# Expert blocks of mixed widths (96, 64 and 32 slots side by side) in a mixture-of-experts stage

## What is computed

```python
scores = sigmoid(h @ w_router)
_, idx = lax.top_k(where(expert_mask, scores + router_bias, -inf), TOP_K)   # 8 of 64, from 4 of 8 groups
gate   = scores at idx, divided by their sum, times 2.5
for each expert e, for the tokens that chose it:
    y = (silu(h @ w_gate[e]) * (h @ w_up[e])) @ w_down[e]
    out[token] += gate * y
out += (silu(h @ ws_gate) * (h @ ws_up)) @ ws_down                          # a shared expert, all tokens
x = rmsnorm(x + g2 * out, final_g)
```

## Time and profile before

| | |
|---|---|
| median of 3 runs | 1466.32 us (1465.88 to 1468.25) |
| the profiled execution | 1468.9 us, span 1467.2 us |
| TensorE busy | 1426.4 us, 97% of the span |
| granted TensorE clock, mean | 0.993 |
| the stage of experts, from the first `gate_up` | 951 us to 1455 us |
| loads from HBM in the middle of that stage | 417 to 422 GB/s |

### The profile page before, as it was taken

The page is one execution under the profiler, slowest core; times in us unless marked ns, Lnnn a source line. Parts: engine busy times, 40 slices in busy tenths (PEclk is TensorE's granted clock), DMA queues, the critical chain, the costliest instruction groups (busy, mean ns, idle before and its releaser), DMA issues.

```text
span 1467.2 us, 17841 instructions
## 1 busy us (share of the span) xinstructions
PE 1426.4 (97%) x6990; PEld 887.1 (60%) x6990; DVE 457.5 (31%) x1035; ACT 210.9 (14%) x515; POOL 67.5 (5%) x101
## 2 busy tenths in 40 slices
PE   8999999999999999999999999999999999999985
PEld 7676585675658867577575675744454445444542
DVE  1136442422542355242245063422111111111113
ACT  2135200000002331000012141200000000000001
POOL 1016200000000010000000000000000000000000
PEclk9999999999999999999999999999999999999997
DMA  9721174464264335664634405589999999998993
GB/s 394 293 82 59 58 275 184 143 245 184 86 229 145 115 116 213 248 254 183 243 148 158 152 21 207 206 346 378 421 421 404 422 421 421 418 421 331 422 421 157
DMA packets 51833, 368.45 MB, mean 251 GB/s; under 512 B 5856, under 2 KB 6064, under 8 KB 7984
## 3 DMA queue, kind: packets, MB, share of 16 engines
q1 hardware_dynamic: 46080, 333.57, 57.0%
q0 software_dynamic: 5392, 32.05, 6.0%
q10 hardware_dynamic: 288, 1.80, 0.3%
HBM read 366.32 MB, written 1.05 MB: 250 GB/s over the span
## 4 chain that ended last, share of the span: by engine, by line
PE 86%; DVE 3%; DMA 1%; issue 0%; ACT 0%; SPq 0%; DVEq 0%
PE ps L833 15%; PE ps L815 13%; PE ps L1222 13%; PE ps L1172 7%; PE ps L1246 6%; PE ps L1204 6%; PE ps L771 6%; PE ps L656 5%; PE ps L732 2%; PE ps L661 2%; PE ps L701 2%; DMA vec_rows<-in_stream 1%; PE ps L794 1%; PE ps L1015 1%; PE ps L1122 1%; PE ps L628 1%
## 5 line engine op out<-in xcount | busy, mean ns | idle before, releaser
L833 PE MATMUL ps<-ring,qk_tiles 128*128 128x512 f32 x512 | 221.4, 592 | 0.0
L815 PE MATMUL ps<-xT,ring 128*128 128x256 f32 x896 | 194.7, 379 | 0.0
L815 PEld LDWEIGHTS ps<-xT,ring 128*128 128x128 f32 x896 | 170.1, 190 | 25.6 <-issue 2.9
L833 PEld LDWEIGHTS ps<-ring,qk_tiles 128*128 128x128 f32 x512 | 97.1, 190 | 118.1 <-issue 117.7
L1222 PE MATMUL ps<-ring,masked_and_probs 128*32 128x512 f32 (+2 forms) x488 | 150.9, 603 | 0.4 <-DMA par<-in_stream 0.4
L1172 PEld LDWEIGHTS ps<-masked_and_probs,mix_rows 128*128 128x128 f32 x896 | 102.5, 192 | 20.8 <-issue 20.8
L656 PE MATMUL ps<-xT,ring 128*128 128x256 f32 x496 | 110.6, 385 | 0.8 <-DVE xT L1666 0.8
L1172 PE MATMUL ps<-masked_and_probs,mix_rows 128*128 128x128 f32 x896 | 107.0, 278 | 0.0
L656 PEld LDWEIGHTS ps<-xT,ring 128*128 128x128 f32 x496 | 95.4, 193 | 14.5 <-issue 1.2
L1204 PE MATMUL ps<-masked_and_probs,probT 128*128 128x512 f32 x216 | 97.2, 593 | 1.0 <-DVE masked_and_probs L2213 1.0
L1246 PE MATMUL ps<-ring,probT 128*32 128x512 f32 (+2 forms) x264 | 83.7, 597 | 1.6 <-DVE probT L2208 1.6
(11 more groups left out here) (387 smaller groups left out, 1699.8 us busy)
## 6 DMA issues: line engine op xcount, KB each, us to landing
ring<-in_stream SPq DMA_DIRECT2D x205, 1024.0 KB, 7.2
qk_tiles<-in_stream SPq DMA_DIRECT2D x48, 1024.0 KB, 14.4
vec_rows<-in_stream SPq DMA_DIRECT2D x13, 1024.0 KB, 14.5
con<-in_stream SPq DMA_DIRECT2D x13, 1024.0 KB, 14.5
qk_tiles<-in_ada POOLq DMA_DIRECT2D x12, 1024.0 KB, 6.0
y_rows<-in_stream SPq DMA_DIRECT2D x12, 1024.0 KB, 13.4
par<-in_stream SPq DMA_DIRECT2D x12, 1024.0 KB, 15.8
xT<-in_stream SPq DMA_DIRECT2D x12, 1024.0 KB, 16.6
```

Of the source, the lines that this page charges most:

```text
L815: mm = pe.matmul(ps[:, bank, (m % 2) * T:(m % 2 + 1) * T], w[:, kk, m * P:(m + 1) * P], xT[:, k, :], start=bank not in started, stop=k == ...
L833: mm = pe.matmul(ps[:, q, :], hT[:, k, t * P:(t + 1) * P], ws[k // 2][:, k % 2, half * 512:(half + 1) * 512], start=k == 0, stop=k == 7)
```

## The change

Four things, all in the stage of experts.

1. **Capacities.** `FIXED` goes from 6 to 3, and the fixed experts get 96 slots. Then come 2 positions of 128 slots, 3 of 96, 21 of 64 and 32 of 32; 61 experts are in the 25 blocks and 3 (`LATE` = 61) are left for the loop.
2. **Kinds of blocks.** A block may hold experts of different widths: `F` is a fixed expert of 96 slots and one of 32 (3 blocks), `M` a ranked expert of 96 and one of 32 (3 blocks), `T` one of 64 and two of 32 (1 block); `S` is one of 128 (2 blocks), `P` two of 64 (10) and `Q` four of 32 (6), as before. An expert of 96 slots is computed as two tiles, of 64 and 32 columns, with the same weights.
3. **Block 0.** The fixed part (96 slots) is gathered as before; its expert of 32 slots is known only after sorting, so its selection, a second gather (`gather_rest`, 16 matmuls of 32 columns) and its copy to `hg` are new. They stand in the middle of the shared expert's down part, whose loops are turned around for it.
4. **Loads.** The 9 chunks of the three fixed experts are loaded first, all others in the order of use; each takes the place that is released in that order (`LOADS`, `SLOT_OF`).

```diff
-FIXED = 6
+FIXED = 3
 UNIT = 32
-POSITIONS = {1: 6, 2: 10, 4: 32}
-LATE = NEXP - PER_MORE
-BLOCK_EXPERTS = [2, 2, 2, 4, 4, 2, 2, 1, 2, 2, 4, 2, 2, 4, 1, 2, 2, 4, 2, 2, 1, 2, 4, 4, 1]
+WIDTHS = ((3 * P // 4, FIXED), (P, 2), (3 * P // 4, 3), (P // 2, 21), (P // 4, 32))
+LATE = FIXED + sum(n for _, n in WIDTHS[1:])
+KINDS = {"F": ((0, 1), (4, 1)), "S": ((1, 1),), "M": ((2, 1), (4, 1)), "P": ((3, 2),), "T": ((3, 1), (4, 2)),
+         "Q": ((4, 4),)}
+BLOCKS = "FFQFQPMSMQTPQPPSPPQPPQPPM"
...
+            for _ in range(n):
+                experts.append([(lo, P // 2), (lo + P // 2, P // 4)] if width == 3 * P // 4 else [(lo, width)])
+                lo += width
...
+LOADS = sorted(USES, key=lambda u: not (BLOCKS[u[0]] == "F" and u[2] == 0))
+for _n, _u in enumerate(LOADS):
+    SLOT_OF[_u] = ((SLOT_ORDER[_n], 1) if _n < MOE_SLOTS else
+                   (SLOT_OF[USES[_n - MOE_SLOTS]][0], SLOT_OF[USES[_n - MOE_SLOTS]][1] + 1))
...
+            def gather_rest():
+                rest = slice(3 * P // 4, P)
+                for k, t in [(k, t) for k in range(KT) for t in range(TT)]:
+                    mm = pe.matmul(ps[:, 6, k * 32:(k + 1) * 32], h2[:, t, k * P:(k + 1) * P], select[:, 0, t, rest],
+                                   start=t == 0, stop=t == TT - 1)
+                mm.then_inc(s_rest, 1)
...
-            for k in range(2):
-                for t in range(TT):
+            for t in range(TT):
+                for k in range(2):
                     for half in range(2):
                         mm = pe.matmul(ps[:, 2 * t + half, :], shactT[:, k, t * P:(t + 1) * P],
                                        w[:, k, half * 512:(half + 1) * 512], start=k == 0, stop=False, skip_group_check=True)
+                if t == 0:
+                    pe.wait_ge(s_selrest, 1)
+                    gather_rest()
             mm.then_inc(s_used, 1)
+            pe.wait_ge(s_hgrest, 1)
...
-                        for a in range(n_experts):
-                            cols = slice(a * width, (a + 1) * width)
-                            mm = pe.matmul(ps[cols, 4, :], hg[:, k, cols], ws[a][:, kk, :], start=k == 0, stop=k == KT - 1,
-                                           skip_group_check=True)
+                        for a, tiles in enumerate(experts):
+                            for lo, width in tiles:
+                                cols = slice(lo, lo + width)
+                                mm = pe.matmul(ps[cols, 4, :], hg[:, k, cols], ws[a][:, kk, :], start=k == 0,
+                                               stop=k == KT - 1, skip_group_check=True)
...
+            select_ranked(0, 0, 1).then_inc(s_selrest, 1)
+            dve.wait_ge(s_rest, 1)
+            dve.tensor_copy(hg[:, :, 3 * P // 4:P], ps[:, 6, 0:256].rearrange("p (k c) -> p k c", k=KT)).then_inc(s_hgrest, 1)
```

More of the change, by code:

```diff
@@ L88, in schedule @@
 def schedule():
[L90 to L97, removed]
+    at = [sum(n for _, n in WIDTHS[:row]) for row in range(len(WIDTHS))]
+    out = []
+    for kind in BLOCKS:
+        parts, experts, lo = [], [], 0
+        for row, n in KINDS[kind]:
+            width = WIDTHS[row][0]
+            parts.append((width, at[row], n))
+            at[row] += n
+            for _ in range(n):
+                experts.append([(lo, P // 2), (lo + P // 2, P // 4)] if width == 3 * P // 4 else [(lo, width)])
+                lo += width
+        assert lo == P
+        out.append((parts, experts))
+    assert at[:-1] == [sum(n for _, n in WIDTHS[:row + 1]) for row in range(len(WIDTHS) - 1)] and at[-1] == LATE
     assert MAX_MORE * PER_MORE + PER_MORE <= UNITS_MAX
@@ L103 @@
 NB = len(SCHEDULE)
+UNIT_TILES = [[(UNIT * i, UNIT)] for i in range(PER_MORE)]
 STATIC = 3 * LATE
+USES = [(b, c, a) for b, (_, experts) in enumerate(SCHEDULE) for c in range(3) for a in range(len(experts))]
+LOADS = sorted(USES, key=lambda u: not (BLOCKS[u[0]] == "F" and u[2] == 0))
+SLOT_OF = {}
+for _n, _u in enumerate(LOADS):
+    SLOT_OF[_u] = ((SLOT_ORDER[_n], 1) if _n < MOE_SLOTS else
+                   (SLOT_OF[USES[_n - MOE_SLOTS]][0], SLOT_OF[USES[_n - MOE_SLOTS]][1] + 1))
 LOOPED = 3 * PER_MORE
 BEFORE_LOOP = STATIC - MOE_SLOTS
-LOOP_ORDER = [(BEFORE_LOOP + n) % MOE_SLOTS for n in range(LOOPED)]
+LOOP_SLOTS = [SLOT_OF[u] for u in USES[BEFORE_LOOP:BEFORE_LOOP + LOOPED]]
 PARAMS = [
@@ new lines, in expert_ids @@
+                return list(ids)
+            experts = None
+            for n, (b, c, a) in enumerate(LOADS):
+                slot = SLOT_OF[b, c, a][0]
+                if n == 3 * FIXED:
+                    sp.wait_ge(s_sched, 1)
+                if n >= 3 * FIXED and b != experts:
+                    experts = b
+                    ids = [0] if BLOCKS[b] == "F" else []
+                    for _, at, n_experts in SCHEDULE[b][0][len(ids):]:
+                        ids = ids + expert_ids(slice(at, at + n_experts), n_experts)
+                if n >= MOE_SLOTS:
+                    sp.wait_ge(*used(n - MOE_SLOTS))
+                elif slot < RING:
+                    sp.wait_ge(s_used, RINGED - RING + (slot - RINGED) % RING + 1)
+                elif slot == VEC_SLOT:
+                    sp.wait_ge(s_normed, 4)
+                elif slot == Y_SLOT:
+                    sp.wait_ge(s_turn, TURN_AT["rms2"] + 4)
+                elif slot == XT_SLOT:
+                    sp.wait_ge(s_used, FIRST["shared"] + 2)
+                elif slot == PAR_SLOT:
+                    sp.wait_ge(s_chosen, TT)
+                else:
+                    sp.wait_ge(s_odone, UNITS[-1][6] + 1)
+                load(slot, RINGED + 3 * SCHEDULE[b][0][0][1] + c if n < 3 * FIXED else ids[a] * 3 + (RINGED + c))
@@ L600, in _ @@
                         sp.wait_ge(s_late, it * LOOPED + (n + 1))
-                        load(SLOT_ORDER[LOOP_ORDER[n]], ids[a] * 3 + (RINGED + c))
+                        load(LOOP_SLOTS[n][0], ids[a] * 3 + (RINGED + c))
             for t in range(TT):
@@ L1207, in scatter, with gate_up @@
                             mm.then_inc(s_moe, 1)
-            def gate_up(n_experts, slots, counts):
-                width = P // n_experts
+            def gate_up(experts, slots, counts):
+                n = len(experts)
                 for c in range(2):
                     ws = []
-                    for a in range(n_experts):
-                        slot, full = slots[c * n_experts + a]
+                    for a in range(n):
+                        slot, full = slots[c * n + a]
                         pe.wait_ge(m_full[slot], full)
@@ L1233, in turn_expert, with down @@
                 mm.then_inc(s_tps, 1)
-            def down(n_experts, slots, buf, counts):
-                width = P // n_experts
+            def down(experts, slots, buf, counts):
+                n = len(experts)
                 ws = []
-                for a in range(n_experts):
-                    slot, full = slots[2 * n_experts + a]
+                for a in range(n):
+                    slot, full = slots[2 * n + a]
                     pe.wait_ge(m_full[slot], full)
@@ L1244, in down @@
                     for half in range(2):
[L1245 to L1249, removed]
+                        for a, tiles in enumerate(experts):
+                            for lo, width in tiles:
+                                mm = pe.matmul(ps[lo:lo + width, 5 + half, :],
+                                               probT[:, buf, k * P + lo:k * P + lo + width],
+                                               ws[a][:, k, half * 512:(half + 1) * 512], start=k == 0, stop=k == 1,
+                                               skip_group_check=True)
                             if k == 1 and half == 1:
-                                mm.then_inc(counts[2 * n_experts + a], 1)
+                                mm.then_inc(counts[2 * n + a], 1)
             def plan_units(n):
@@ L1267, in plan_units @@
                     pe.matmul(ps[0:1, 7, P:2 * P], ecol[E], pick, start=True, stop=True).then_inc(s_urank, 1)
[L1269 to L1272, removed]
+            for n, (_, experts) in enumerate(SCHEDULE):
+                first = USES.index((n, 0, 0))
+                slots = [(slot, 16 * loads) for slot, loads in (SLOT_OF[u] for u in USES[first:first + 3 * len(experts)])]
+                counts = [used(first + i)[0] for i in range(3 * len(experts))]
                 pe.wait_ge(s_hga, n + 1)
@@ L1276, in _ @@
                     pe.wait_ge(s_hid2, n)
-                gate_up(n_experts, slots, counts)
+                gate_up(experts, slots, counts)
                 pe.wait_ge(s_sel, n + 2)
@@ L1293, in _ @@
                 pe.wait_ge(s_hgv, n + 2)
-                down(n_experts, slots, n % 2, counts)
+                down(experts, slots, n % 2, counts)
                 plan_units(n)
@@ L1301, in _ @@
             with pe.Fori(0, more) as it:
-                slots = [(SLOT_ORDER[i], it * 16 + 16 * ((STATIC - i - 1) // MOE_SLOTS + 2)) for i in LOOP_ORDER]
```

(35 more changed lines are left out.)

70 lines of the change are left out of this document (22 added, 48 removed).

## The result

| | before | after |
|---|---|---|
| median, us | 1467.01 (4 runs, 1465.88 to 1468.25) | 1540.64 (4 runs, 1536.23 to 1545.64) |
| span of the profiled execution, us | 1467.2 | 1538.4 |
| TensorE busy in it, us | 1426.4 | 1503.9 |
| bytes read from HBM | 366 MB | 357 MB |

The ratio is 1.049, with a 95% interval of 1.047 to 1.051: the changed kernel is 4.9% slower, though it reads less. The forecast was 1535 us.

A forecast was written before the change was run, and what follows sets the result against it. TensorE's work was taken to bound the kernel: 1468.9 us, less 24.4 (loop pass removed, block 0 added), plus 93 for mixed widths, less 2.6 for the median, gave 1535 us. Its own range was 1524 to 1556, the whole range 1438 to 1556.

The forecast's parts named there:

- What bounds the kernel: Expert stage: TensorE's work is the chain from first gate_up to first loop pass; only the second pass hangs on a load.
- One loop pass: Loop: by the router's token counts, 4 units remain instead of 8, so one pass instead of two.
- The stretch removed, 27.9 us: Loop: one pass less saves 27.9 us, some 19 of work and 9 of the load and slow gate_up behind it.
- the third rival: Loop still makes two passes: 1553 us or a little more with the forecast's widths, 1477 with free widths; chance 0.03.
- Block 0, 3.5 us: Shared down part: gather_rest adds 32 passes, 3.5 us on TensorE's path, with its two waits covered; bounds 0 to 4.5.
- Mixed widths, 93 us: Seven F, M, T blocks: 64- and 32-column tiles can't run side by side, 13.3 us more each, 93 in all.
- alternating ones: Mixed blocks: a tile's two passes not issued together, widths alternating pass by pass, 46 changes, 16.3 us a block, 114 in all.
- The sum: Whole kernel: 1468.9 - 24.4 + 93 = 1537.5 us, less 2.6 for the median, say 1535.
- free mixing: Rival for mixed blocks: tiles of two widths on different columns overlap freely, 1442 us; chance 0.18.
- cheap changes: Rival for mixed blocks: each width change costs 0.13 us but tiles overlap, 2.9 us a block, 1462 us; chance 0.04.

The follow-up runs named there:

- before_mixed: Kernel before, with the second expert's 64 slots in 7 two-expert blocks computed as two tiles of 32 columns, the first staying one of 64: 1558.36 us.
- all32: Changed kernel with every expert of the 7 mixed blocks (F, M, T) computed in tiles of 32 columns: 1446.53 us, ratio 0.985 to the kernel before.
- one96: Changed kernel with each expert of 96 slots computed as one tile of 96 columns instead of 64 and 32: 1548.51 us, one run.
- grouped: Changed kernel with the wide tiles of each half of gate_up first, then the narrow ones, and down likewise: 1519.59 us, one run.
- all32_pass: all32 with one more loop pass, forced by a table, that computes nothing used: 1474.33 us, ratio 1.004 to the kernel before.

## Why the prediction was right, point by point

- **What bounds the kernel**: right. TensorE's work is the chain from the first `gate_up` to the loop in every version, with a load in it only where there is a second pass, and each us added to a block came out whole.
- **One loop pass**: right, counted from the router's output; 1503.58 is the only pass.
- **The stretch removed, 27.9 us**: right in size (26.6 in the trace with the pass put back, 26.4 to 27.8 by the medians). Its reason was half wrong. I took the wait for loads as an effect of the many loads ahead, and so expected slower blocks to remove it (before_mixed). It stood unchanged (TensorE idle for 6.2 us in both, behind a load of 20.28 us), because the pass waits for places that the pass before holds; the time that slower blocks give can't be used, since only 17 chunks have a place. So the third rival, two passes at 1535 + 18 us, was priced some 9 us too low. And the slow half of `gate_up`, which I left without a cause, is the lower clock behind the wait.
- **Block 0, 3.5 us**: right. L1227 and L1203 together are 10.64 us for 7.07 of L1196 before, 3.6 us more, with both waits hidden.
- **Mixed widths, 93 us**: right. From block 0's start to the end of the loop's first `gate_up` it is 1510.45 - 957.10 = 553.35 us, for 1411.43 - 951.03 = 460.40 before: 92.95 us for seven blocks, 13.3 each. The issue of two passes of a tile together (four rounds and two changes in a step), which I preferred over alternating ones, is what the timeline shows.
- **The sum**: 92.95 - 27.85 + 3.57 + 2.52 = 71.2 us, the difference of the spans. The 2.52 us were not in it. They stand ahead of the first gather (941.68 for 939.16), and 1.6 of them are a stretch of lower clock; the rest is within what that point differs by from trace to trace. The other 3 us between 1535 and the median of 1540.64 are that I took 2.6 us off for the median of before, while that of the changed kernel lies 0.5 above its profiled execution. The row of each kernel for it, the changed one first:

```profile
935.00:938.00 3.00, 3.00 (x18) 2.79 (x18) 1.36 (x5) 0.00 (x0) 0.00 (x0) 0.61 0.03 5
935.00:938.00 3.00, 3.00 (x29) 3.00 (x29) 0.98 (x4) 0.00 (x0) 0.00 (x0) 1.00 0.86 360
```

  The columns are those of the earlier trace rows; the granted clock is 0.61 in the one and 1.00 in the other, and the same 32 passes took 5.40 us for 3.77. Such a stretch at the lower of the two levels (1.2 for 2.4 GHz), behind the same work, is at this place in the traces of three kernels (the changed one, all32 and one96), and not in those of grouped and all32_pass, whose order of work there is the same. It comes and goes between executions, so I ascribe it to no edit; whether the changed kernel gets it more often is open. Its runs spread wider than those of before beside them (9 us for 2), but 13 later runs of the kernel before spread over 8 us as well, the longest (1473.77) at a mean granted clock of 0.987, the shortest (1465.76) at 0.995.
- **The rivals**: free mixing fell, and cheap changes with it. Free mixing was the span rule for packed tiles of the Trainium skill (TensorE: Matmul & The Clock Gate, Part 3) read without a condition. The traces give it for one width only: 0.01 us from tile to tile. The Trainium skill (TensorEngine Tiling (Array Packing), Tiling Modes) has the condition, that changing the mode drains TensorE. The traces agree with it: 0.134 us for a change, and no overlap between the widths. That the array empties is still a reading of the rows; what they show is when passes start and when weights are loaded.

## What to carry to other kernels

When matmuls are packed side by side on the columns of the array, give all tiles of a step the same width: cut a 96-column operand into three of 32, not into 64 and 32. Extra tiles of that width were free here, a second width more than doubled the step (1.98 us for 0.86). And look in the trace of before for what a change of shape does at the places where it already happens (one row of 0.52 us among rows of 0.43 was enough); a small price at a border can be the sign of a large one inside a loop. Last, in a loop whose loads wait for its own places, each pass behind the first pays for their time, and a wait can cost more than its length when the clock falls in it: removing one pass was worth 28 us, 10 more than its work, 2 of them the clock.

## What the runs showed of the hardware

- Passes of 32 columns wait for passes of 64 on other columns, and their weight loads wait too; a change of width costs 0.134 us besides. I had not expected how exactly this is additive: 13.28 us a block in the changed kernel, 13.3 forecast from rows of before.
- A tile of 96 columns beside one of 32 behaves as two widths (16.04 us). In blocks of one width, the 64 passes of a `gate_up` in 32-column tiles take as long as the 32 passes in 64-column ones (7.00 and 7.02 us).
- Four tiles of one expert pair streaming the same weights two by two: no cost (ratio 1.000, 0.999 to 1.002).
- While TensorE waited 6.2 us for a load its granted clock fell to 0.50, and the next rounds took 0.85 us for 0.43.
